# Block 1's output on one Trainium2 core: the norm weights loaded earlier, tile 0's projection placed between the rows' spreads

## The reference

```python
merged = (gates[..., :D_MODEL] * (ret_y.astype(dt) @ w_ret_out_l)
          + gates[..., D_MODEL:] * (gdn_y.astype(dt) @ w_gdn_out_l))
mixer_out = merged.astype(dt) @ w_o_l
...
x = x + g1 * _rmsnorm(mixer_out, norm_mix_post[i])
h2 = _rmsnorm(x, norm_ffn_pre[i]) * (1.0 + sc2) + sh2
x = x + g2 * _rmsnorm(_moe(h2, *moe_p), norm_ffn_post[i])
```

## Time and profile before

| | |
|---|---|
| three runs | 3138.81, 3148.53, 3137.05 us; median 3138.81 |
| profiled execution | 3138.8 us, its span 3137.1 us |
| mean granted TensorE clock | 0.948 of full |
| PE busy | 2718.1 us (87%) |
| DVE, ACT, POOL busy | 930.9, 459.9, 502.2 us |
| chain that ended last | PE 59%, DMA 25%, DVE 9%, issue 4% |
| DMA | 793.01 MB, mean 253 GB/s |

### The profile page before, as it was taken

The page is one execution under the profiler, slowest core; times in us unless marked ns, Lnnn a source line. Parts: engine busy times, 40 slices in busy tenths (PEclk is TensorE's granted clock), DMA queues, the critical chain, the costliest instruction groups (busy, mean ns, idle before and its releaser), DMA issues.

```text
span 3137.1 us, 37076 instructions
## 1 busy us (share of the span) xinstructions
PE 2718.1 (87%) x15537; PEld 1332.3 (42%) x15537; DVE 930.9 (30%) x1540; ACT 459.9 (15%) x1005; POOL 502.2 (16%) x383
## 2 busy tenths in 40 slices
PE   5998699989989899989999597785998888888887
PEld 2545577744435554544445233443333233233232
DVE  2044555521133411111111486843111211111112
ACT  2022233201022111111111202421000000000001
POOL 0001233302001243434443101201000000000000
PEclk8999899989989999999999798896999999999999
DMA  5110254523123599989998410035999999999996
GB/s 234 54 54 0 79 169 156 162 118 121 54 99 150 205 381 381 377 329 356 365 354 322 179 54 24 24 135 196 429 427 427 428 427 427 427 428 428 427 427 278
DMA packets 99820, 793.01 MB, mean 253 GB/s; under 512 B 18738, under 2 KB 19122, under 8 KB 53704
## 3 DMA queue, kind: packets, MB, share of 16 engines
q1 hardware_dynamic: 74824, 743.92, 58.1%
q0 software_dynamic: 23008, 37.81, 5.0%
q10 hardware_dynamic: 1824, 8.91, 0.7%
HBM read 768.99 MB, written 38.86 MB: 258 GB/s over the span
## 4 chain that ended last, share of the span: by engine, by line
PE 59%; DMA 25%; DVE 9%; issue 4%; ACT 2%; POOL 1%; SPq 0%; POOLq 0%; ACTq 0%; DVEq 0%
DMA arena<-in_w_down 13%; PE b L3009 9%; DMA yd<-arena 6%; PE b L1903 6%; PE b L1467 5%; PE b L509 4%; DMA arena<-h2d,arena 3%; PE b L1917 3%; PE b L3044 3%; PE b L511 3%; PE b L2494 2%; PE b L3024 2%; PE b L1531 2%; PE b L1485 2%; DVE arena L2540 2%
## 5 line engine op out<-in xcount | busy, mean ns | idle before, releaser
L3009 PE MATMUL b<-arena 128*64 128x512 f32 x2048 | 452.4, 599 | 20.3 <-DMA arena<-in_w_up 11.2
L1903 PE MATMUL b<-arena 128*64 128x256 f32 x3072 | 355.3, 383 | 2.4 <-DVE arena L2186 1.3
L3009 PEld LDWEIGHTS b<-arena 128*64 128x64 f32 x2048 | 155.6, 137 | 311.2 <-issue 275.7
L3024 PE MATMUL b<-arena 128*64 128x512 f32 x1024 | 232.2, 597 | 63.7 <-DMA arena<-in_w_down 50.3
L1903 PEld LDWEIGHTS b<-arena 128*64 128x64 f32 x3072 | 212.8, 137 | 113.9 <-issue 4.5
L2220 POOL DMA_INDIRECT yd<-arena x96 | 152.5, 1589 | 344.8 <-ACT arena L2001 115.0
L1917 PE MATMUL b<-arena 128*64 128x512 f32 x768 | 187.4, 609 | 0.7 <-issue 0.7
L2176 DVE TENSOR_TENSOR arena<-arena,b 128x128 f32<-128x128 f32 x96 | 27.8, 290 | 516.1 <-ACT arena L1994 478.6
L1467 PE MATMUL b<-arena 128*128 128x512 f32 x384 | 168.2, 600 | 9.3 <-DMA arena<-in_w_in 9.3
L3024 PEld LDWEIGHTS b<-arena 128*64 128x64 f32 x1024 | 71.5, 136 | 223.5 <-issue 112.7
L3116 DVE TENSOR_TENSOR arena<-arena,b 128x512 f32<-128x512 f32 x32 | 20.6, 686 | 460.7 <-PE b L3009 460.7
(11 more groups left out here) (481 smaller groups left out, 3399.5 us busy)
## 6 DMA issues: line engine op xcount, KB each, us to landing
arena<-in_w_gu SPq DMA_DIRECT2D x65, 2048.0 KB, 8.0
arena<-in_w_gate SPq DMA_DIRECT2D x64, 2048.0 KB, 30.5
arena<-in_w_up SPq DMA_DIRECT2D x64, 2048.0 KB, 30.0
arena<-in_w_down SPq DMA_DIRECT2D x63, 2048.0 KB, 24.9
arena<-in_w_dn SPq DMA_DIRECT2D x65, 1024.0 KB, 10.0
arena<-in_w_mod SPq DMA_DIRECT2D x80, 512.0 KB, 3.8
arena<-in_w_in SPq DMA_DIRECT2D x19, 2048.0 KB, 8.0
arena<-yd SPq DMA_DIRECT2D x12, 512.0 KB, 7.8
```

Of the source, the lines that this page charges most:

```text
L1903: x = e.matmul(ps[i % 2][64 * j:64 * j + 64, 0:256], XGT[i % 2][:, k % 4, (k // 4) * 64:(k // 4) * 64 + 64], GUB[place_of(w)][:, k, j * 25 ...
L3009: x = e.matmul(ps[b + c][64 * hf:64 * hf + 64, :], XS[q % 2][:, kb, (n % 2) * 64:(n % 2) * 64 + 64], w[:, at_w:at_w + 512], start=(kb == 0 ...
L3024: x = e.matmul(ps[4][64 * hf:64 * hf + 64, :], H[:, c * 4 + j, hi * 64:hi * 64 + 64], w[:, i * 1024 + hf * 512:i * 1024 + hf * 512 + 512], ...
```

## The change

It consists of two edits in `mixer_out`. `gains` gets another place: 4096 columns at `K.base1`, where `HT` was, and its load is issued right behind chunk 8, with no wait of its own. And TensorE's list has spreads 0 and 1, the first half of tile 0's projection, spreads 2 and 3, the second half, and then `rows.done`. `wo` takes the halves that it shall make.

```diff
-    gains = GT[:, :, 1024:2048]
+    gains = K.area(K.base1)(4096).rearrange("p (t n) -> p t n", t=4)
...
             e.dma_start(wr[n % 3], chunks[n]).then_inc(*came_w[n % 3].up(n))
+            if n == 8:
+                e.dma_start(gains, I["gains"]).then_inc(*came_gain.up("out"))
...
         e.dma_start(wr[1], I["w_in_2"][3]).then_inc(*came_w[1].up("k"))
-        e.wait_ge(*mm.at("mt", 3, 1))
-        e.dma_start(gains, I["gains"]).then_inc(*came_gain.up("out"))
...
-        for n in range(4):
-            rows.spread(e, n)
+        rows.spread(e, 0)
+        rows.spread(e, 1)
+        wo(e, 0, (0,))
+        rows.spread(e, 2)
+        rows.spread(e, 3)
+        wo(e, 0, (1,))
         rows.done(e)
-        wo(e, 0)
...
-    def wo(e, t):
-        for c in range(2):
+    def wo(e, t, cs=(0, 1)):
+        for c in cs:
```

## The result

| | before | changed |
|---|---|---|
| median of 20 runs each | 3147.12 us (3134.91 to 3154.14) | 3127.51 us (3115.34 to 3138.29) |
| ratio | | 0.9943, 95% interval 0.9933 to 0.9954 |
| profiled execution | 3138.8 us, span 3137.1 | 3134.3 us, span 3132.7 |

The change makes the kernel faster by 0.57%, which of 3147.12 is 17.9 us (14.5 to 21.1). Forecast were 18.4 us, and 3120.4 us for the whole, which is 7.1 us under what was measured. The two medians lie 19.6 us apart; the ratio is the better measure, and by it the gain was about right while the base was not: of the kernel before only three runs were known, with a median of 3138.81, and twenty runs have it at 3147.12. That the gain came out so near is partly luck, since at the changed place itself 2.2 us are missing, as the profile shows.

The account below looks back on a forecast made before the run. The prediction took one late load, the norm weights, to bound block 1's output; 34.3 us would become 15.9, so 3138.8 - 18.4 = 3120.4 us, 0.59% less, with a range of 3115 to 3129 us.

Parts of the forecast that it names:

- What bounds the place: Block 1's output: one late norm-weight load, landing 13.8 us after issue; VectorE waits 13.2 us, TensorE 11.8 us.
- rival 5: VectorE still waits for the norm weights, so nothing is gained: 3138.8 us; chance 0.01.
- The issue of the load, priced at nothing: SP's norm-weight load moves from 880.46 to about 817.8, costs nothing, with 50 us of cover.
- The new sum of 15.9 us: TensorE from first spread to block 2's first spread: 15.9 us against 34.3, so 18.4 us less.
- the term for the clock: TensorE's granted clock at tile 0's first half: no fall taken; both ends 0 and 2.6 us.
- the row at 976: Earlier trace: spreads, 1.45 us idle, eight transposes, then clock 0.55, costing 1.78 us; its quiet part was longer.
- rival 1: A stretch of low clock at tile 0's first half, costing 1.8 to 2.6 us: 3122.2 to 3123.0 us; chance 0.17.
- The rule on transposes: Skill page: transposes don't engage full clock, so the projection would begin slow; the prediction said the trace speaks against it.
- The reload's slack of 0.4 us: Modulation rows' reload before block 2's spreads lands at 896.8, wanted at 897.20; nothing taken, up to 3 us in range.
- rival 2: The modulation rows' reload becomes the wait: 7 us landing, 2.4 us idle, 1.8 of low clock; 3124.6 us; chance 0.06.
- Handed on whole: Behind the place nothing runs by its own timetable, so the 18.4 us shift reaches the end whole.
- Rivals 3 and 4: 3: a later stage keeps part, 3129.4 us, chance 0.06; 4: expert-stage gathers served later, slower, 3149.2 us, chance 0.04.

Follow-up runs that it names:

- order alone: Changed kernel with the norm weights again loaded behind the last transpose, TensorE's new order kept; ratio 0.9968 to the kernel before.
- 13.8 us more: Changed kernel with tile 0's first half made three times, the last one counting; ratio 0.9991 to the kernel before.
- rows last: Changed kernel with spreads 2 and 3 moved behind the second half of tile 0's projection; 3133.2 us in its one run.
- the gap kept: The product in front, but waiting for all eight merged-token copies before tile 0's first half; 35.88 us from first of the last transposes to first norm transpose.
- the product in front: Changed kernel with tile 0's first half directly behind the transposes and tile 1's first half ahead of rows.done; ratio 0.9949 to the kernel before.

## Why the prediction was right or wrong

**What bounds the place: right.** L336's wait for the norm weights has gone (so rival 5 did not come), and no other wait took its place. With the early load alone it is gone too, and with the new order alone it is still there: the wait was the load's.

**The issue of the load, priced at nothing: right.** It lands at 823.49 + 13.5 = 837.0, and TensorE is busy for all of the 42 us up to the last transposes:

```profile
840.00:882.00 42.00, 42.00 (x99) 18.50 (x98) 12.44 (x18) 0.00 (x0) 0.00 (x0) 1.00 0.00 0
```

**The new sum of 15.9 us from the first spread to block 2's: it was 18.06** (905.06 - 887.00). Spreads 1.14 and 1.07 against twice 1.07, right. Second half 7.08 against 6.88. First half 8.77 against 6.88: this is the step that failed, the term for the clock, put at nothing. I weighed the row at 976 and took no fall, because the quiet part would be shorter here (1.95 us against 3.5). The clock fell to its low level in the first half in both profiles of the changed kernel, and cost 1.9 us, within the 1.8 to 2.6 that rival 1 had. It is no matter of chance: in the three other kernels that have the same gap and the same two spreads in front of tile 0's first half (order alone, 13.8 us more, rows last), it falls there as well (means over 3.5 us of 0.52, 0.53 and 0.57) and costs about 1.9 us: five profiles of five. Rival 1 was the case that came, and of the 18.4 us 16.2 were got. The choice between the two ends was wrong, the ends were right. Both places of the earlier trace rows where the clock fell, behind 880.40 and behind 976, had spreads in front of them, which I weighed for one of them only; at the first I put the fall down to the hole.

**The rule on transposes.** Rival 1 came, but not by that rule. Behind the same transposes the clock is 1.00 where dense work follows, with the gap (the gap kept, 884.8 to 892.0) and without it (the product in front, 876 to 910). The Trainium skill's page "TensorE: Matmul & The Clock Gate" (Part 4: PE-mode transpose) would have the clock low there too; the trace disagrees.

**The reload's slack of 0.4 us: right** (0.3), and what it costs uncovered is 6.95 us. The 7 us landing of rival 2 did not come.

**Handed on whole: right as far as it can be measured.** 13.76 us more at the place came out as some 15 of the whole, give or take 6.

**Rivals 3 and 4** were both in question after the first profiles, with 5 to 6 us more behind the place. Twelve profiles show the stage behind to scatter by more than that, and the ratio gives 17.9 us for the whole against 16.2 to 16.9 in D: nothing was kept or added that could be seen. The interval of the gain, 14.5 to 21.1 us, would still allow some 2 us kept or 4 to 5 added.

**The absolute time: 7.1 us too low.** The second step that failed is the base of the sum: one profiled execution and three runs, at 3138.8. Twenty and twenty-seven runs of the kernel before, in the two largest comparisons, have medians of 3147.12 and 3144.68. The base was 8.3 us low, and the medians lie 19.6 us apart where 18.4 were forecast; that leaves the 7.1. The ratio forecast was 0.9941, measured 0.9943. So near a hit is luck: its interval is three times as wide as the 2.2 us by which the place missed. The line of 15.7 us at 3123.1 hung on the same base; 3127.51 lies above it, and the kernel is faster all the same, since twenty runs of each give the ratio to 0.1%.

## What to carry to other kernels

Where a late load ends a wait, look for a place that falls free earlier, and then ask what the next wait is: here 4.7 of the 16.2 us came only with the new order, from VectorE's reads and the low clock that went with them, of which the profile before showed 1.43 us of issue as a hole. Put short spreads between dense products, not in a row and not behind a gap; at this place that was seen in D and E, not in the time of the whole. And forecast the difference or the ratio rather than the time: a median of three runs was eight microseconds off where the stages scatter.

## What the runs showed of the hardware

Where TensorE's clock fell at this place, spreads with two rows stood in front of it. Two of them behind 0.88 us of idle time were followed by a fall to 0.50 (0.52 to 0.57 as the mean over 3.5 us) in both profiles of the changed kernel, and in three other kernels too; each time it cost about 1.9 us. Four in a row with no gap in front were followed by 0.52 in one profile; whether the two-row products or the pauses between them did it is open. In one profile 0.83 us of idle time with a dense product behind was not (1.00), nor were two spreads between dense halves (7.08 us against 6.88 for the half that follows, with the clock at 1.00). Why such a half takes 0.2 us more is not settled; it does so behind every pair of spreads, and the half behind the 0.83 us gap took 7.12.

The last transposes of the kernel began between 876.0 and 883.4 us in twelve profiles whose work up to there was the same but for one load, and the wait at the middle loop of block 1's experts was 7.7 us once and 14.6 to 15.9 us in the other eleven.
